# One wait moved on GpSimd, and turns and attention steps placed one to three half tiles earlier

## What is computed

```python
# three dilation groups g, 16 heads of 64
k, v = split(rms_norm(x, kv_norm) @ kv_w)            # 1024 -> 2 * 3 * 1024
q = rms_norm(x, b_norm) @ b_w_q                      # 1024 -> 3 * 1024
q, k = rope(rms_norm(q, q_gain)), rope(rms_norm(k, k_gain))   # by head
for g, (window, dilation) in enumerate(((128, 1), (512, 4), (2048, 16))):
    o[g], lse[g] = masked_softmax_attention(q[g], k[g], v[g])
out = sum(softmax(lse)[g] * o[g] for g in range(3)) @ w_o
```

## Time and profile before

| | |
|---|---|
| median of 3 runs | 1830.65 us (1828.43 to 1831.77) |
| the profiled execution's own time | 1830.65 us |
| its span | 1828.8 us |
| TensorE busy | 1756.2 us, 96% |
| VectorE, ScalarE, GpSimd busy | 62%, 49%, 15% |
| chain that ended last, by engine | PE 81%, DVE 10%, ACT 4%, POOL 2% |
| mean granted TensorE clock | 0.989 of full speed |

### The profile page before, as it was taken

One profiled execution on the slowest core, in us unless ns is written; L12 is line 12 of the kernel. 1 busy time (PEld: TensorE's weight loads), 2 busy tenths in 40 slices (PEclk: granted clock), 3 DMA queues, 4 the chain that ended last, 5 costly groups with the idle time before them and its releaser, 6 DMA issues.

```text
span 1828.8 us, 23188 instructions
## 1 busy us (share of the span) xinstructions
PE 1756.2 (96%) x9397; PEld 1485.2 (81%) x9397; DVE 1125.0 (62%) x1395; ACT 896.4 (49%) x1049; POOL 281.2 (15%) x210
## 2 busy tenths in 40 slices
PE   8899999999988999999999999999999999999997
PEld 6787999977766787999988888788888887878886
DVE  6567655588775865555564676365555677556554
ACT  6465544465544554544455545554445544554442
POOL 3820000038943710000012000000002000000000
PEclk9999999999998999999999999999999999999999
DMA  8336555545622443555565555255555446435651
GB/s 290 135 115 202 174 190 195 185 139 163 201 74 93 139 173 116 184 196 185 187 205 182 177 214 182 95 184 185 184 185 192 161 176 230 147 127 196 194 186 69
DMA packets 160635, 311.10 MB, mean 170 GB/s; under 512 B 5692, under 2 KB 53313, under 8 KB 159761
## 3 DMA queue, kind: packets, MB, share of 16 engines
q1 hardware_dynamic: 158512, 299.33, 49.2%
q0 software_dynamic: 2016, 10.29, 1.5%
HBM read 304.35 MB, written 5.24 MB: 169 GB/s over the span
## 4 chain that ended last, share of the span: by engine, by line
PE 81%; DVE 10%; ACT 4%; issue 2%; POOL 2%; DMA 1%; DVEq 0%; SPq 0%; ACTq 0%; POOLq 0%
PE ps L454 21%; PE ps L456 21%; PE ps L455 21%; PE ps L673 4%; PE ps L674 4%; PE ps L675 4%; PE ps L417 4%; DVE wlo L1422 3%; ACT whi L946 2%; DVE work L1559 1%; DVE nw L1474 1%; PE ps L910 1%; ACT work L1043 1%; DVE st L1503 1%; DVE nw L1475 1%
## 5 line engine op out<-in xcount | busy, mean ns | idle before, releaser
L1422 DVE TENSOR_TENSOR wlo<-raw,whi 128x2048 fp32r<-128x2048 f32 x279 | 659.2, 2369 | 440.7 <-ACT whi L946 440.6
L454 PE MATMUL ps<-whi,hT_hi 128*128 128x512 f32 x1936 | 764.3, 395 | 11.3 <-DVE wlo L1422 4.9
L456 PE MATMUL ps<-whi,hT_lo 128*128 128x512 f32 x1936 | 753.2, 389 | 0.0
L455 PE MATMUL ps<-wlo,hT_hi 128*128 128x512 f32 x1936 | 752.4, 389 | 0.0
L946 ACT ACTIVATE whi<-raw 128x2048 fp32r<-128x2048 f32 x279 | 533.8, 1914 | 394.6 <-PE ps L456 336.5
L454 PEld LDWEIGHTS ps<-whi,hT_hi 128*128 128x128 f32 x1936 | 365.2, 189 | 91.0 <-issue 10.6
L456 PEld LDWEIGHTS ps<-whi,hT_lo 128*128 128x128 f32 x1936 | 364.6, 188 | 76.3
L455 PEld LDWEIGHTS ps<-wlo,hT_hi 128*128 128x128 f32 x1936 | 365.4, 189 | 70.7
L673 PE MATMUL ps<-hT_hi,whi 128*128 128x256 f32 x640 | 183.6, 287 | 0.0
L674 PE MATMUL ps<-hT_lo,whi 128*128 128x256 f32 x640 | 182.1, 284 | 0.0
L675 PE MATMUL ps<-hT_hi,wlo 128*128 128x256 f32 x640 | 181.9, 284 | 0.0
(11 more groups left out here) (198 smaller groups left out, 1182.2 us busy)
## 6 DMA issues: line engine op xcount, KB each, us to landing
raw<-in_w_in SPq DMA_DIRECT2D x46, 1024.0 KB, 5.1
raw<-in_w SPq DMA_DIRECT2D x88, 512.0 KB, 4.7
raw<-in_m_w_up SPq DMA_DIRECT2D x32, 1024.0 KB, 5.3
raw<-in_m_w_down SPq DMA_DIRECT2D x32, 1024.0 KB, 4.8
raw<-in_kv_w SPq DMA_DIRECT2D x24, 1024.0 KB, 5.2
raw<-in_w SPq DMA_DIRECT2D x22, 1024.0 KB, 4.8
raw<-in_b_w_q SPq DMA_DIRECT2D x12, 1024.0 KB, 5.1
raw<-in_a_w_qkv SPq DMA_DIRECT2D x11, 1024.0 KB, 7.0
```

Source lines behind the costliest of these rows:

```text
L454: pe.matmul(acc, xh, wh, start=start and k == 0, stop=False)
L455: pe.matmul(acc, xh, wl, start=False, stop=False)
L456: ins = pe.matmul(acc, xl, wh, start=False, stop=stop and k == kc - 1)
L1422: vec.tensor_tensor(wlo[:, m % SPLIT, :], raw[:, m % RAW, :], whi[:, m % SPLIT, :], ALU.subtract).then_inc(*mark("lo_ready", ("lo", m)))
```

## The change

```diff
-        B_STEPS = (40, 74)
-        B_TURNS = {13: (0, 0, 0), 18: (0, 0, 1), 23: (0, 1, 0), 28: (0, 1, 1), 33: (0, 2, 0), 39: (0, 2, 1),
-                   46: (1, 0, 0), 49: (1, 0, 1), 54: (1, 1, 0), 59: (1, 1, 1), 66: (1, 2, 0), 73: (1, 2, 1)}
+        B_STEPS = (39, 71)
+        B_TURNS = {13: (0, 0, 0), 18: (0, 0, 1), 23: (0, 1, 0), 28: (0, 1, 1), 33: (0, 2, 0), 38: (0, 2, 1),
+                   46: (1, 0, 0), 49: (1, 0, 1), 54: (1, 1, 0), 58: (1, 1, 1), 65: (1, 2, 0), 70: (1, 2, 1)}
...
                     settle(pool, g_.tensor_tensor(d_a, d_a, d_b, ALU.add), name, *key, "r1")
-                    pool.wait_ge(*at("rqk", *key[1:3]))
                     g_.tensor_tensor(src, d_a, norm, ALU.mult).then_inc(*mark(name, key))
...
                         pool.wait_ge(*at("sq", i, s, t))
+                        pool.wait_ge(*at("rqk", i, s))
                         rotate(heads(qk_raw[s][:, t, :]), heads(rope_a), heads(rope_b), bc(tabs[:, 0, ti, t], 1, 8),
```

## The result

The changed kernel takes 1839.36 us (median of 5 runs, 1837.95 to 1840.56) against 1830.61 us before (1828.43 to 1831.77, 5 runs): a ratio of 1.0055, 95% interval 1.0044 to 1.0066. Over all 22 executions of the changed kernel the times run from 1837.95 to 1842.40 with a median of 1840.3; the profiled one took 1841.55 us, its span is 1839.7. The time lies outside the range of the forecast (1815 to 1836), on the side of its third rival and 3.5 us beyond that.

A forecast was written before the change was run, and what follows sets the result against it. TensorE's matmuls were taken to set the pace, with at most about 37 us to be had. Losses 3.4 + 0.5 + 3.5, gains 8.1 + 5.1 + 0.3: 6.1 us faster than 1830.65, 1824.5 (range 1815 to 1836).

The forecast's parts named there:

- third rival: Both halves' last turns stall, TensorE waiting 6.2 and 5 us, and the clock falls: 1835.9 us; chance 0.20.
- 0.5 + 3.5 = +4.0: Half 1's products: 0.5 us lost at turns moved from 59 and 66, 3.5 at the last turn, moved three places.
- half 1's steps: Sums behind whole tiles, no split ahead: 5.6 us idle and 2.0 slow clock fall to about 2.5; 5.1 gained.
- memory's scaling: Scaling of the memory's rows stands behind shorter scales: 0.3 us gained.
- The turns moved from places 59 and 66 by one place each: Half 1's turns, each moved one place earlier, lose 2.8 of about 3 us of slack: 0.5 us lost (0 to 2).
- Key block 2's rotation starts at 482.3 and ends at 500.6: Half 0, GpSimd: rotation starts only at its scales, about 482.3 instead of 481.12, and ends at 500.6 (499.9 to 503.2).
- 3.4 us lost: Half 0's last turn, moved to tile 19's middle: TensorE there at 497.0, waits 3.6 us; net 3.4 lost.
- the 2.5 of the forecast: A query block's scales on VectorE, with GpSimd otherwise idle, fall from 4.1 to 2.5 us.
- 8.1 gained: Half 0's steps: TensorE's waits, slow clock and meetings with rotations sum to 15.8 us against 23.9; range 2 to 14.
- the walk through VectorE's order: Half 0's steps, step 7 and its copy now ahead of the scales: TensorE's waits come out at 9.4 us.
- the 14 that I had named as the sign of being wrong: Half 0's steps: prediction is wrong if TensorE's idle time there stays above 14 us.
- the rival in which VectorE bounds the steps: VectorE alone bounds half 0's steps; their chain starts as late as before, ends 2 us sooner: 1832.8 us; chance 0.23.

The follow-up runs named there:

- The two experiments on this turn: Changed kernel with turn 58 put back to 59: 1830.53 us; kernel with moved wait, steps from 73, last turn 72, with turn 59 moved to 58: 1833.55 us.
- the turn at 58 (first fence): Against the kernel with moved wait, half 1's steps from 73 and last turn at 72: turn moved from 59 to 58; 1833.55 us.
- the turn at 59 (second fence): Against the kernel before: wait moved, half 1's steps from 73 instead of 74, its last turn at 72 instead of 73; 1825.02 us.
- the places of the version with slack: Against the kernel before: half 1's steps from 73 instead of 74, its last turn at 72 instead of 73, wait as before; 1825.66 us.

## Why the prediction was wrong

Two ledgers. The first is by place, from the two profiled executions: how much later than before the changed kernel is, which the terms of the prediction's sum give too (10.9 us at the end by the executions' own times).

| stretch | predicted | measured |
|---|---|---|
| up to half 0's first scores | +3.4 | +9.5 |
| half 0's steps | -8.1 | -6.6 |
| half 1's products, to its first scores | 0.5 + 3.5 = +4.0 | +12.7 |
| half 1's steps | -5.1 | -4.5 |
| memory's scaling | -0.3 | none |
| sum | -6.1 | +11.1 |

So by place both gains came nearly as forecast, and the turns were under-priced, by 6.1 and 8.7 us. The first and last rows of TensorE that the steps are measured by, changed kernel, half 0 and half 1:

```profile
510.48 1.15 PE L591 MATMUL ps<-wide 64*128 64x256 f32 x12
...
583.90 0.42 PE L617 MATMUL ps<-work,nat 128*64 128x128 f32 x4
...
667.45 1.15 PE L591 MATMUL ps<-wide 64*128 64x256 f32 x12
...
726.49 0.39 PE L617 MATMUL ps<-work,nat 128*64 128x128 f32 x4
```

Half 0's steps took 73.8 us, and 74.8 up to the first product behind the turn that now follows them, against 81.4; half 1's 59.4 against 63.9 (660.2 to 724.1). The start at 510.48 is at place 39; before, the steps began at 503.75 at place 40, one half tile (2.8) later in the work: 6.7 + 2.8 = 9.5 late. In half 1 it is 667.45 - 660.2 + 3 x 2.8 = 15.6 late, of which 2.9 were there after half 0.

The second ledger is by edit, from the runs: each kernel is one step further towards the changed one. The differences are between medians, each against runs of the kernel before beside it, and each median ratio has an interval of 1.6 us or more to either side; so a step is good to about 2 us, and only the last row is told from nothing.

| edit | predicted | measured |
|---|---|---|
| the wait, old places | -0.3 | -1.6 |
| half 0's places | 3.4 - 8.1 = -4.7 | +1.6 |
| half 1's steps, turns 65 and 70 | 3.5 - 5.1 = -1.6 | +0.7 |
| turn 59 to 58 | 0.5 | +8.1 |

**The step that failed most: "The turns moved from places 59 and 66 by one place each lose 2.8 of about 3 us of slack; 0 to 2 lost, I take 0.5."** The two experiments on this turn give 8.1 and 9.1 us, each kernel taken against the kernel before on its own chip (8.8 and 8.5 between the medians themselves). Two things were wrong in it. The slack was less: with the moved wait and the old places the turn at 59 already waits 1.4 us, since key block 1's rotation is stretched by splits as that of block 2 is, for which I had worked it out; I did not apply to half 1 what I had found in half 0. And the wait was priced at its own length, though its place decides what stands behind it. Neither is enough alone: with the old wait the turn at 58 doesn't wait, and all of half 1's new places together come to +1.0 (1830.56 against 1829.55).

**"Key block 2's rotation starts at 482.3 and ends at 500.6", and "3.4 us lost" by it.** GpSimd's timeline, changed kernel, first instructions of key block 1 and of key block 2, and VectorE's sum of key block 2's squares:

```profile
448.75 3.19 POOL L2001 TENSOR_TENSOR work<-work 128x512 f32<-128x512 f32 x1 [0.83 <-DVE rqk L1476]
...
485.71 3.21 POOL L2001 TENSOR_TENSOR work<-work 128x512 f32<-128x512 f32 x1 [2.09 <-DVE rqk L1476]
```

```profile
480.04 1.22 DVE L1503 TENSOR_REDUCE st<-work 128x16 f32<-128x1024 f32 x1 [2.62 <-ACT work L1096]
```

The rotation takes 18.3 us, as worked out, but starts 3.4 us late. Key block 1's, 18.5 us from 448.75, made TensorE wait 2.52 us at place 28, in the middle of key block 2's first tile (14). TensorE came there 1.3 us earlier than before (not 2.7) and left 1.2 later, and the next seven or so products started 0.43 us apart instead of 0.23: the squares of key block 2 are summed at 480.04 instead of 477.19. Of these 2.85 us about 1.6 are the slow clock, which not every execution has (last section). Query block 2, whose last tile is 13, was not delayed by this wait; but its scales took 4.0 us (465.14 to 469.16) and not the 2.5 of the forecast, since key block 1's rotation, up to 467.23, stood beside them. GpSimd was not idle there. The wait at place 38 was 5.7 us and not 3.6, and a slow clock followed that the sum hadn't priced: the turn takes 1.97 us instead of 1.09, and the window from 504 to 512 has a clock of 0.65.

**"8.1 gained" in half 0's steps** was 6.6. The 6.12 us wait is gone, as the walk through VectorE's order had it, but it left out ScalarE (2.3 us for the exponentials, L1043), and had 2.7 us for the second sum, which waits 3.97 us at 556.5. TensorE's idle time in this stage is 15.7 us, above the 14 that I had named as the sign of being wrong; the clock is what became better. And the new places in half 0 brought no net gain by the ledger of edits. With the wait alone the steps start 5.1 us late, at 508.81, and end only 0.9 late, at 586.1: 77.3 us already. With half 0's places alone they take 76.3 (507.54 to the first product behind the turn, 583.8). A late start is mostly caught up within the steps, whichever edit made it late. That is the rival in which VectorE bounds the steps, in part; that VectorE is what holds the end was not tested.

**Right.** The scales of half 0's first query block and of half 1's three fell to 2.5 us (the other two of half 0 took 3.3 and 4.0). The first instruction of a rotation that meets a split takes 3.18 to 3.21 us, and key blocks' rotations take 18.2 to 18.6 us, query blocks' 14.3 to 15.2 beside products, against 18.3 and 14.5 worked out; the rule that I weighed, one port pair held as a lock (the Trainium skill, "SBUF — State Buffer", "SBUF: two separate sides"), agrees with these rows. L1579 fell as forecast. The third rival had the sign, the two waits of 5.7 and 2.8 us (it said 6.2 and 5) and the slow clock behind both; it did not have place 58, which carries the loss.

## What to carry to other kernels

A wait is not priced by its length alone but by what its engine still has to do behind it: ask of every place at which a wait may appear whether the next block's last work stands behind it, and put it behind that work if it can stand there. When two edits share one slack, price each with the other in place; here each alone was within 2 us and together they cost 8.8. A delay found for one block of a repeated pattern holds for every block of it, so walk all of them, not the one next to the edit.

## What the runs showed of the hardware

TensorE fell to its lower clock behind waits of 2.5 and 4.1 us in a stretch of otherwise dense products, where the sum had it only in the steps. With the turn at 58 (first fence) the window behind the first has 0.76, that behind the second 0.79; with the turn at 59 (second fence) the wait of 1.37 us leaves 1.00:

```profile
611.00:618.00 7.00, 6.82 (x27) 5.88 (x28) 0.00 (x0) 3.10 (x6) 0.13 (x1) 0.76 0.34 129
...
624.00:632.00 8.00, 7.37 (x30) 6.25 (x31) 7.27 (x7) 4.17 (x6) 7.84 (x5) 0.79 0.40 131
```

```profile
613.00:620.00 7.00, 6.55 (x32) 5.26 (x32) 5.68 (x16) 3.70 (x5) 2.56 (x3) 1.00 0.37 140
```

The length of a single wait doesn't tell it: before, 2.99 us at 620 stand in a window at 1.00. Nor does the program tell it. With the wait alone the turn at place 28 waits as in the changed kernel, behind the same instructions, and the clock stays up; TensorE's turn and the window behind it, then that window in the changed kernel:

```profile
467.20 1.09 PE L417 MATMUL ps<-ident,work 128*128 128x128 f32 x8 [2.41 <-POOL work L2008]
```

```profile
467.00:473.00 6.00, 5.80 (x30) 4.96 (x31) 3.95 (x11) 2.95 (x3) 3.92 (x3) 1.00 0.10 15
```

```profile
467.00:473.00 6.00, 5.71 (x22) 4.71 (x23) 4.05 (x11) 1.27 (x3) 3.91 (x3) 0.72 0.08 16
```

Seven of the kernels are one program up to here and wait 2.39 to 2.57 us at this turn: three of their profiled executions have 0.72 behind it, four 1.00. In the same way the split's wait of 2.35 to 2.41 us at 416 leaves 1.00 in the kernel before and in the places of the version with slack, 0.72 or 0.73 with all places, half 1's or half 0's places alone. Such a fall costs about 1.6 us, so a difference of that size at one place between two single executions is no proof of what an edit does. What decides stays open here.

And GpSimd's instructions were late by one split at most, even where VectorE has two in its queue back to back: in the changed kernel L2001 has 1.27, 1.31 and 3.23 us as its shortest, median and longest of 32.
